# A two-layer block with a dilated attention: the next projection begun inside the feed-forward, groups kept as tops and sums in the order 16, 4, 1, and two token tiles merged inside the last attention

## The chip, the cores and the metric

The kernel runs on one core of one Trainium2 chip. The metric is the device time of one execution in microseconds. The kernel before took 2705.37 us, the median of 3 runs (2704.56 to 2706.03).

## The reference

The input x has 1024 tokens of 1024 float32 values. Two layers follow each other. Layer 0 mixes tokens with a gated linear attention, layer 1 with a dilated window attention; each layer then has a cross attention over 256 memory rows, an output projection, and a feed-forward with a depthwise convolution. What matters here:

```python
def reference(x, mem, positions, ...):
    mem_n = rms_norm(mem, mem_norm)
    for i in range(2):
        h = rms_norm(x, mix_norm[i])
        tok, xq = gla_mixer(h, ...) if i == 0 else dilated_mixer(h, b_w_in, b_q_norm, b_k_norm, positions)
        xa = memory_cross_attention(xq, mem_n, xa_w_kv[i], xa_q_norm[i], xa_k_norm[i])
        x = x + jnp.concatenate([tok, xa], axis=-1) @ w_out          # 512 + 256 columns in layer 1
        x = x + conv_ffn(rms_norm(x, ffn_norm[i]), ffn_w_up[i], ffn_conv_w[i], ffn_conv_b[i], ffn_w_down[i])
    return x

def dilated_mixer(h, w_in, q_norm, k_norm, positions):
    q, k, v, xq = split_cols(h @ w_in, [1536, 1536, 1536, 256])
    q, k = normed and rotated, 12 heads of 128
    for g, (window, dilation) in enumerate(((128, 1), (512, 4), (2048, 16))):     # 4 heads each
        o, lse = dilated_window_attention(q[g], k[g], v[g], window, dilation)     # lse = m + log(l)
    wts = jax.nn.softmax(jnp.stack(lses), axis=0)
    return jnp.sum(wts[..., None] * jnp.stack(outs), axis=0), xq
```

m is the largest score of a row, l the sum of exp(score - m), and o is normalised by l.

## The kernel before

Tokens lie in 8 tiles of 128. Every float32 matrix product is made of three products of rounded parts, high x high, high x low and low x high (`split_matmul`, L50 to L52), so each weight is loaded raw, its high part is copied by the scalar engine (ACT) and its low part subtracted by the vector engine (DVE), or both are made by GpSimd (POOL). The program is a row of phases (`p0`, `gla`, `o0`, `f0`, `p1_0`, `da0`, `p1_1`, `da1`, `p1_2`, `da2`, `o1`, `f1`); each is one block with an instruction stream per engine, written out by hand with semaphores, and ends in a barrier of all engines. So in each phase every engine works in its program's order, and nothing of a phase starts before the one ahead has ended.

`ffn_phase` runs 11 groups. The last one (`down_group`, 16 psum banks of 512 columns, banks 4 to 7 in turn) multiplies the down weights; DVE adds each bank to x (L256), and a bank is used again when it was added four banks later. In `f0` the norm for layer 1 is made beside it: ACT squares and scales a tile (L421, L426), POOL makes the root (L431, L433), PE turns it (L453), DVE applies the gain (L463), ACT makes the high and DVE the low part (L469, L475). The down weights' last parts (L195, L249) come ahead of it.

`project_phase` multiplies the normed rows with blocks of weights, in groups of three token tiles, each block in two halves of rows (`kh`). In a "heads" block ACT squares each head (L982), POOL makes the root (L1015, L1017), DVE scales (L1046) and rotates (L1062 to L1068), PE turns the heads one group later (L1088) and ACT copies them out (L994). A block's weights are split by ACT (L803) and DVE (L808) ahead of the tiles of the last group of the block before; the high part of the first half waits until the last group has read the old ones. The first block of `p1_0` is the memory query of layer 1, 256 columns (its raw weights are loaded during `f0`, and split at the phase's start); then come q, k and v, 512 columns each.

`attention_phase` runs one unit for each token tile and head (32 for a dilated group; `da0` has 32 more for the memory attention): PE makes the scores (L1179), DVE masks them and finds the top (L1208), ACT takes the exponential and its sum (L1230), PE turns the probabilities (L1187), DVE copies them (L1216) and inverts the sum (L1217), PE multiplies with the values (L1196), ACT scales the result with the inverse (L1239). PE turns unit i - 2 and multiplies unit i - 3 while it scores unit i. A group ends with Ln of the sums on ACT (L1242) and a subtraction on DVE (L1220). SP stores the outputs of four units at a time to DRAM, in the order of tokens, and the logarithms (L2278). POOL splits weights for what comes next: two chunks of the next q block, or three of the six chunks of the output projection (L545, L547). The groups run with dilation 1, 4, 16.

`out_phase` of layer 1 (`o1`) splits the other weight chunks, loads the logarithms and, tile by tile, the three groups' outputs, forms the weights (`Merge.dve_weights`, L1965 to L1975) and the weighted sum (`Merge.dve_add`: 4 operations at L1986, 8 at L1988), turns the merged tile (L719), splits it (ACT L625, DVE L665), and multiplies it with the output weights: 36 matmuls of 512 columns a tile. Then it adds x and makes the norm of the feed-forward.

Of the kernel before, what the change touches and what calls it, by code (L numbers as in the profile page):

```python
# [27 lines left out]
P = 128  # L28
# [49 lines left out]
def ffn_phase(nc, ph, psum, ident, neg_half, X, hT_hi, hT_lo, w_up, conv_w, conv_b, w_down, x_out, raws, up, next_gain=None, next_w=None):  # L78
# [3 lines left out]
    with ExitStack() as ctx:  # L82
# [15 lines left out]
        taps_rows = sb("taps_rows", [2 * FC, 4, P])  # L98
        taps = sb("taps", [P, 4, 2 * FC])

# [48 lines left out]
        def _(sp):  # L149
# [19 lines left out]
            for j in range(2 if next_w else 0):  # L169
                sp.wait_ge(up_split, 2 * FC - 2)  # L170
                raws.load(sp, j, next_w[j])
# [6 lines left out]
        def _(act):  # L178
# [44 lines left out]
            high_last_down()  # L223
            if norm:
# [10 lines left out]
        def _(dve):  # L235
# [26 lines left out]
            def group(g, par, last=False):  # L262
# [29 lines left out]
                if not is_first(g):  # L292
                    add_group(g - 1, range(8, 12))
                    if last:
                        low_last_down()
                    add_group(g - 1, range(12, 2 * TT))
# [19 lines left out]
        def _(pe):  # L316
# [52 lines left out]
            if norm:  # L369
                for t in range(TT - LAG, TT):  # L370
                    norm.pe(pe, t)

        for j in range(2):
            raws.count[j] += 16 * (FC - 1 + (next_w is not None))
# [107 lines left out]
class OutWeights:  # L482
# [3 lines left out]
    def __init__(self, nc, ctx, ph, chunks, w_out, raws, ahead):  # L486
# [6 lines left out]
        self.before = list(raws.count)  # L493
        for k in range(chunks):
# [22 lines left out]
    def load_ahead(self, sp, k):  # L517

        if k < min(self.ahead + 2, self.chunks):
            self.load(sp, k)  # L520
# [40 lines left out]
def out_phase(nc, ph, psum, ident, neg_half, XY, weights, x_dram, gain, out_hi, out_lo, w_up, up, raws, stage=None):  # L561
# [3 lines left out]
    with ExitStack() as ctx:  # L565
# [8 lines left out]
        y_hi = [x[:, 0:chunks, :] for x in up.hi]  # L574
        y_lo = [x[:, 0:chunks, :] for x in up.lo]
# [12 lines left out]
        merge = Merge(nc, ctx, ph, stage, XY) if stage is not None else None  # L588
# [3 lines left out]
        def _(sp):  # L592
            for k in range(weights.ahead + 2, (chunks - 1 if merge else chunks) if weights.stage is None else 0):
                weights.load(sp, k)
            if merge:
                stage.wait_logs(sp)
                merge.load_logs(sp)
                stage.wait_outputs(sp)
                merge.load(sp, 0)
                for k in range(max(weights.ahead + 2, chunks - 1), chunks):  # L600
                    weights.load(sp, k)
                merge.load(sp, 1)
            for j in range(2):
# [1920 lines left out]
```

## Time and profile before

| | |
|---|---|
| runs | 2705.37 us median (2704.56 to 2706.03) |
| profiled execution | 2706.76 us, its span 2704.9 us |
| PE matmul busy | 2596.7 us |
| DVE busy | 1317.2 us |
| ACT busy | 845.6 us |
| POOL busy | 185.9 us |

Busy is the time in which the engine has an instruction in work. Matmuls overlap each other, so the distance between the starts of two, and not their duration, is what one costs. A wait row names the instruction that waited, then what ended the wait, and the sum, number and longest of the waits. PEq is PE's own sequencer: a wait put down to it here is the start of a phase.

### The profile page before, as it was taken

Reading aid. Unit: us, or ns where it says so; the run is one execution under the profiler, and the core shown is the slowest. Engines: PE = TensorE matmul, PEld = TensorE weight load, DVE = VectorE, ACT = ScalarE, POOL = GpSimd, SP = SyncE. Lnnn points to the kernel's source line nnn. Section 1 sums busy time; section 2 is a strip of 40 time slices with the busy share of each in tenths; the row PEclk is TensorE's granted clock in tenths of the full one; section 3 lists DMA queues with packets and bytes.
Section 4 is the critical chain, followed back from the end, with each engine's and each line's share of the span. In section 5 each row is a group of like instructions: output and inputs, shape, how many; then the busy total and the mean of one; then the engine's idle time right before and its main releaser. Section 6 shows DMA issues by size and latency. Waiting matters only on the chain. (4 is left out here: it accounts for less than half of the span.)

```text
span 2704.9 us, 33076 instructions
## 1 busy us (share of the span) xinstructions
PE 2596.7 (96%) x12444; PEld 2201.6 (81%) x12444; DVE 1317.2 (49%) x2306; ACT 845.6 (31%) x1782; POOL 185.9 (7%) x263
## 2 busy tenths in 40 slices
PE   7998888999999999998999999997999999999999
PEld 7997767888888888887888888796778888888887
DVE  4423463354445555545545553443645444544455
ACT  6434342332222222224326433324332222222221
POOL 1100120000000000002211111111000000000000
PEclk9999898999999999998999999998999999999999
DMA  4221301131111111102102001103421111111111
GB/s 145 89 71 26 99 6 50 36 96 47 47 47 51 50 47 47 47 32 101 58 6 75 32 32 55 55 16 103 140 65 55 60 49 47 49 52 47 47 39 63
DMA packets 165245, 153.88 MB, mean 57 GB/s; under 512 B 32856, under 2 KB 135496, under 8 KB 165128
## 3 DMA queue, kind: packets, MB, share of 16 engines
q1 hardware_dynamic: 160968, 152.31, 17.7%
q8 instruction: 72, 1.18, 0.2%
q10 hardware_dynamic: 4160, 0.02, 0.1%
q14 instruction: 45, 0.37, 0.1%
HBM read 134.69 MB, written 17.61 MB: 56 GB/s over the span
## 5 line engine op out<-in xcount | busy, mean ns | idle before, releaser
L356 PE MATMUL psum<-hT_hi,f_up_hi 128*128 128x512 f32 x1376 | 426.7, 389 | 4.6 <-PEq L565 3.9
L356 PE MATMUL psum<-hT_hi,f_up_lo 128*128 128x512 f32 x1376 | 426.3, 389 | 0.0
L356 PE MATMUL psum<-hT_lo,f_up_hi 128*128 128x512 f32 x1376 | 426.2, 389 | 0.0
L238 DVE TENSOR_TENSOR f_up_lo<-raw,f_up_hi 128x1024 fp32r<-128x1024 f32 x84 | 102.9, 1225 | 490.6 <-ACT f_up_hi L182 490.6
L356 PEld LDWEIGHTS psum<-hT_hi,f_up_hi 128*128 128x128 f32 x1376 | 258.1, 188 | 59.4 <-issue 5.9
L356 PEld LDWEIGHTS psum<-hT_hi,f_up_lo 128*128 128x128 f32 x1376 | 258.3, 188 | 53.8
L356 PEld LDWEIGHTS psum<-hT_lo,f_up_hi 128*128 128x128 f32 x1376 | 258.3, 188 | 53.6
L256 DVE TENSOR_TENSOR XY<-XY,psum 128x512 f32<-128x512 f32 x352 | 234.4, 684 | 113.9 <-PE psum L52 113.7
L182 ACT ACTIVATE f_up_hi<-raw 128x1024 fp32r<-128x1024 f32 x84 | 89.1, 1061 | 614.6 <-PE psum L356 589.0
L50 PE MATMUL psum<-w_hi,hT_hi 128*128 128x512 f32 (+1 forms) x640 | 250.0, 391 | 17.0 <-DVE w_lo L808 10.5
L50 PE MATMUL psum<-f_down_hi,f_act_hi 128*128 128x512 f32 x640 | 249.0, 389 | 0.0
L51 PE MATMUL psum<-f_down_lo,f_act_hi 128*128 128x512 f32 x640 | 249.0, 389 | 0.0
L52 PE MATMUL psum<-f_down_hi,f_act_lo 128*128 128x512 f32 x640 | 249.0, 389 | 0.0
L52 PE MATMUL psum<-w_hi,hT_lo 128*128 128x512 f32 (+1 forms) x640 | 246.1, 385 | 0.0
L51 PE MATMUL psum<-w_lo,hT_hi 128*128 128x512 f32 (+1 forms) x640 | 246.0, 384 | 0.0
L50 PEld LDWEIGHTS psum<-w_hi,hT_hi 128*128 128x128 f32 x640 | 138.8, 217 | 35.7 <-DVE w_lo L808 10.1
L52 PEld LDWEIGHTS psum<-w_hi,hT_lo 128*128 128x128 f32 x640 | 138.8, 217 | 18.1
L51 PEld LDWEIGHTS psum<-w_lo,hT_hi 128*128 128x128 f32 x640 | 139.1, 217 | 16.7
L52 PEld LDWEIGHTS psum<-f_down_hi,f_act_lo 128*128 128x128 f32 x640 | 120.1, 188 | 25.0
L51 PEld LDWEIGHTS psum<-f_down_lo,f_act_hi 128*128 128x128 f32 x640 | 120.1, 188 | 24.9
L50 PEld LDWEIGHTS psum<-f_down_hi,f_act_hi 128*128 128x128 f32 x640 | 120.1, 188 | 24.9
L50 PE MATMUL psum<-w_hi,h_hi 128*128 128x384 f32 (+1 forms) x320 | 106.1, 332 | 2.3 <-DVE h_lo L475 1.7
(296 smaller groups left out, 4019.5 us busy)
## 6 DMA issues: line engine op xcount, KB each, us to landing
raw<-in_ffn_w_up_dram SPq DMA_DIRECT2D x88, 512.0 KB, 3.7
f_down_raw<-in_ffn_w_down_dram SPq DMA_DIRECT2D x22, 1024.0 KB, 4.9
w_raw<-in_b_w_in_dram SPq DMA_DIRECT2D x18, 1024.0 KB, 5.0
w_raw<-in_a_w_in_dram SPq DMA_DIRECT2D x8, 768.0 KB, 5.8
group_out<-stage SPq DMA_DIRECT2D x24, 256.0 KB, 2.3
o_outs<-group_out SPq DMA_DIRECT2D x24, 256.0 KB, 3.5
XY<-in_x_dram SPq DMA_DIRECT2D x8, 512.0 KB, 10.2
w_raw<-in_xa_w_kv_dram SPq DMA_DIRECT2D x8, 512.0 KB, 3.6
```

Of the source, the lines that this page charges most:

```text
L50: nc.tensor.matmul(out, lhs_hi, rhs_hi, start=start, stop=False)
L51: nc.tensor.matmul(out, lhs_hi, rhs_lo, start=False, stop=False)
L52: return nc.tensor.matmul(out, lhs_lo, rhs_hi, start=False, stop=stop)
L182: nc.scalar.activation(up_hi[n_slot][:, :, :], up_raw[n_slot], ACT.Copy).then_inc(up_high, 1)
L238: nc.vector.tensor_tensor(up_lo[n_slot][:, :, :], up_raw[n_slot], up_hi[n_slot][:, :, :].bitcast(F32), ALU.subtract).then_inc(up_split, 1)
L256: nc.vector.tensor_tensor(xs, xs, psum[:, 4 + i % 4, :], ALU.add).then_inc(x_added, 1)
L356: mm = nc.tensor.matmul(psum[:, 2 * j + half, :], w[j][:, d, :], h[:, d, half * HALF:(half + 1) * HALF], start=first, stop=final)
```

## The change

Three parts.

In `f0` a new helper, `Begun`, loads, splits and holds the memory query's weights, and PE multiplies token tiles 0 to 3 with them in banks 4 to 7 between the last transposes of the norm. `p1_0` finds these four tiles done and computes tiles 4 to 7 with the same weights; its slots for weights now load without waiting for earlier ones.

The dilated groups run in the order 16, 4, 1. Outputs are stored unnormalised, with the tops and the sums in place of the logarithm. Ln, its subtraction and the reciprocals of these units are gone. The weights become exp(-(top - smallest negated top)), divided by the sum over the groups of weight x sum. The last group's tops and sums stay in SBUF.

In the last attention (dilation 1) POOL splits all six chunks of the output weights, the last three after the first tiles' weights are formed. At fixed units DVE forms the weights of token tiles 0 and 1 (units 14 and 16) and merges tile 0 (units 18, 20, 22), PE turns tile 0 into bank 7 (units 10 and 28), and ACT and DVE split it. SP loads the groups' parts of tiles 0 and 1. `out_phase` starts with the matmuls of tile 0 and with the merge of tile 1; SP loads x and the other tiles in a new order.

```diff
@@ ffn_phase
             if norm:
                 for t in range(TT - LAG, TT):
+                    if begin:
+                        if t == TT - LAG:
+                            pe.wait_ge(norm.low, begin.TILES)
+                        for i in begin.between[t - TT + LAG]:
+                            pe.wait_ge(x_added, 2 * TT * GROUPS - begin.TILES + i + 1)
+                            begin.pe(pe, i, psum[:, 4 + i, :], hT_hi, hT_lo)
                     norm.pe(pe, t)
+                for i in begin.between[LAG] if begin else ():
+                    pe.wait_ge(x_added, 2 * TT * GROUPS - begin.TILES + i + 1)
+                    begin.pe(pe, i, psum[:, 4 + i, :], hT_hi, hT_lo)
...
@@ ffn_phase, vector engine
                     if last:
                         low_last_down()
+                        if begin:
+                            begin.low_parts(dve)
                     add_group(g - 1, range(12, 2 * TT))
...
+class Begun:
+    TILES = 4
+    between = ((0,), (1, 2), (3,))
...
+    def pe(self, pe, t, bank, stat_hi, stat_lo):
+        if t == 0:
+            pe.wait_ge(self.split, 2)
+        for d in range(DC):
+            tok = slice(t * P, (t + 1) * P)
+            split_matmul(self.nc, bank[:, 0:self.w.shape[1]], stat_hi[:, d, tok], stat_lo[:, d, tok],
+                         self.hi[d // 4][:, d % 4, :], self.lo[d // 4][:, d % 4, :], d == 0, d == DC - 1)
...
@@ OutWeights
-    def split_ahead(self, pool):
+    def split_ahead(self, pool, merge):
         for k in range(self.ahead):
+            if k == self.ahead // 2:
+                pool.wait_ge(merge.weighed, 1)
...
@@ attention_phase, scalar engine
-                    nc.scalar.activation(out, psum[:, S + T + u % O, 0:w], ACT.Copy, scale=inv[:, u:u + 1]).then_inc(out_done, 1)
-                if i == staged + T_LAG - 1 and staged:
-                    act.wait_ge(inverted, staged)
-                    nc.scalar.activation(total[:, 0:staged], total[:, 0:staged], ACT.Ln).then_inc(logged, 1)
+                    src = psum[:, S + T + u % O, 0:w]
+                    if u < staged:
+                        if u % 4 == 0 and stage.before(u // 4):
+                            act.wait_ge(stage.stored[u // 4 % 2], stage.before(u // 4))
+                        nc.scalar.activation(out, src, ACT.Copy).then_inc(out_done, 1)
...
@@ Merge
+    EARLY = 2
+    TURN_XA, EXP, ADD, TURN = 10, 15, 18, 28
...
+    def dve_ahead(self, dve, i, topped, expd, mixed):
+        if i == self.EXP - 1:
+            dve.wait_ge(topped, self.EARLY * DIL_HEADS)
+            dve.wait_ge(self.logs_loaded, 16 * 2 * (self.G - 1))
+            self.shift(dve, 0, self.EARLY)
+        if i == self.EXP + 1:
+            dve.wait_ge(expd, self.EARLY * DIL_HEADS)
+            self.weigh(dve, 0, self.EARLY)
+        if i == self.ADD:
+            dve.wait_ge(mixed, 2 * DIL_HEADS)
+            dve.wait_ge(self.first_loaded, 16 * 2 * self.G)
+        if self.ADD <= i < self.ADD + 2 * self.G and (i - self.ADD) % 2 == 0:
+            self.add_group(dve, 0, (i - self.ADD) // 2)
+        if i in (self.TURN_XA + 1, self.TURN + 1):
+            part = i == self.TURN + 1
+            dve.wait_ge(self.high, part + 1)
+            self.nc.vector.tensor_tensor(self.turn_rows(self.turn_lo, part), self.turn_cols(part),
+                                         self.turn_rows(self.turn_hi, part).bitcast(F32), ALU.subtract).then_inc(self.low, 1)
...
@@ out_phase, vector engine
             if merge:
-                for k in range(weights.ahead, chunks - 1):
-                    weights.low_part(dve, k)
-                merge.dve_weights(dve)
-                merge.dve_add(dve, 0)
-            y_part(0)
...
+                merge.dve_add(dve, 1)
+                merge.shift(dve, merge.EARLY, TT)
+                merge.weigh(dve, merge.EARLY, TT)
...
@@ build
+        order = [2, 1, 0]
...
-            slots = WeightSlots(nc, slots_ctx, "w", HALF, raws)
+            slots = WeightSlots(nc, slots_ctx, "w", HALF, -2)
```

## Rows read from the trace of the kernel before

**Rows 1.** The page's busy time, share of the span and instructions by engine.
```profile
PE 2596.7 (96%) x12444; PEld 2201.6 (81%) x12444; DVE 1317.2 (49%) x2306; ACT 845.6 (31%) x1782; POOL 185.9 (7%) x263
```

**Rows 2.** Waits of PE, 1190 to 2000 us: total, times, longest.
```profile
PE psum L719 <- DVE XY L1988: 15.6, 1, 15.6
PE psum L50 <- DVE w_lo L808: 10.5, 6, 8.0
PE psum L50 <- PEq L1141: 6.5, 2, 4.8
...
PE psum L1187 <- ACT raw L1230: 2.5, 2, 1.6
PE psum L356 <- PEq L565: 2.2, 1, 2.2
```

**Rows 3.** Windows: busy by engine, PE's granted clock, DMA share, GB/s.
```profile
1248.00:1293.00 45.00, 32.06 (x233) 30.84 (x232) 19.71 (x39) 20.81 (x83) 10.86 (x18) 0.81 0.20 71
1700.00:1705.00 5.00, 4.96 (x15) 4.02 (x16) 0.00 (x0) 0.00 (x0) 0.00 (x0) 0.67 0.44 109
1878.00:1909.00 31.00, 12.71 (x49) 9.87 (x48) 14.23 (x43) 7.99 (x11) 0.00 (x0) 0.67 0.60 180
```

**Rows 4.** Timeline of PE, end of f0 to q block: start, us, instruction.
```profile
1248.39 1.03 PE L453 MATMUL psum<-ident,f_conv_value 128*128 128x128 f32 x8
...
1278.39 0.28 PE L50 MATMUL psum<-w_hi,hT_hi 128*128 128x256 f32 x1
...
1278.75 0.28 PE L50 MATMUL psum<-w_hi,hT_hi 128*128 128x256 f32 x1
...
1292.66 0.47 PE L50 MATMUL psum<-w_hi,hT_hi 128*128 128x512 f32 x1 [1.68 <-DVE w_lo L808]
```

**Rows 5.** Timeline of ACT and DVE, first query tile's head rows.
```profile
1272.47 0.22 ACT L982 ACTIVATE raw<-psum 128x64 f32<-128x64 f32 x1 [9.09 <-PE psum L52]
...
1274.81 0.86 DVE L1046 SCALAR_TENSOR_TENSOR p_head_roped<-psum,p_head_rstd,xa_q_gain 128x64 f32<-128x64 f32 x4 [9.98 <-POOL p_head_rstd L1017]
```

**Rows 6.** Timeline of DVE and PE before f0's last group.
```profile
1217.51 2.35 DVE L249 TENSOR_TENSOR f_up_lo<-f_down_raw,f_up_hi 128x1024 fp32r<-128x1024 f32 x2
...
1222.14 0.39 PE L50 MATMUL psum<-f_up_hi,f_act_hi 128*128 128x512 f32 x1
```

**Rows 7.** Timeline of ACT and SP at the end of da1.
```profile
1696.29 0.35 ACT L1239 ACTIVATE stage<-psum,da_inv 128x128 f32<-128x128 f32 x1
...
1697.03 1.30 SPq L2278 DMA_DIRECT2D group_lse<-stage_lse  x2
```

**Rows 8.** A window of the dilation-1 group, columns as in rows 3.
```profile
1450.00:1461.00 11.00, 11.00 (x83) 9.99 (x82) 8.39 (x41) 8.55 (x30) 4.77 (x2) 1.00 0.16 60
```

**Rows 9.** Timeline of DVE, weights and first merged tile in o1.
```profile
1887.87 0.18 DVE L1965 TENSOR_TENSOR o_top<-o_logs 128x32 f32<-128x32 f32 x1
...
1890.40 0.87 DVE L1986 TENSOR_SCALAR XY<-o_outs,o_logs 128x128 f32<-128x128 f32 x4
1891.31 2.31 DVE L1988 SCALAR_TENSOR_TENSOR XY<-o_outs,o_logs,XY 128x128 f32<-128x128 f32 x8
```

**Rows 10.** Timeline of POOL in da2 and f0, and DVE beside it.
```profile
1850.53 1.04 POOL L545 CAST o_w_hi<-raw 128x1024 fp32r<-128x1024 f32 x1 [51.89 <-DMA raw<-in_b_w_out_dram]
1851.65 2.37 POOL L547 TENSOR_TENSOR o_w_lo<-raw,o_w_hi 128x1024 fp32r<-128x1024 f32 x1
...
1236.43 0.99 POOL L431 TENSOR_SCALAR f_norm_sums<-f_norm_sums 128x1 f32<-128x1 f32 x1 [2.31 <-ACT f_conv_value L421]
...
1236.15 1.22 DVE L475 TENSOR_TENSOR hT_lo<-f_down_raw,hT_hi 128x1024 fp32r<-128x1024 f32 x1
```

**Rows 11.** Timeline of PE, end of da2 and second tile of o1.
```profile
1877.22 0.85 PE L1196 MATMUL psum<-XY,da_buffer 128*128 128x128 f32 x4
...
1909.12 0.50 PE L50 MATMUL psum<-o_w_hi,f_up_hi 128*128 128x512 f32 x1 [0.93 <-DVE f_up_lo L665]
```

**Rows 12.** Chain of waits, 512-column matmuls: start, us, what.
```profile
1997.43 71.03 PE psum L356 x312
```

More of the change, by code:

```diff
@@ L517, in load_ahead @@
     def load_ahead(self, sp, k):
-        if k < min(self.ahead + 2, self.chunks):
-            self.load(sp, k)
+        self.load(sp, k)
     @classmethod
@@ L611, in _ @@
                 sp.dma_start(x_old[:, :], x_dram[t * P:(t + 1) * P, :]).then_inc(x_loaded, 16)
+                if merge and t == 0:
+                    merge.load(sp, 2)
+                    merge.load(sp, 3)
+                if merge and 4 <= t + 3 < TT:
+                    merge.load(sp, t + 3)
+                if t == 2:
+                    for j in range(2):
+                        sp.wait_ge(w_split, chunks)
+                        raws.load(sp, j, up_unit(w_up, j, 0))
         def y_cols(t):
@@ L632, in _ @@
             if merge:
-                for k in range(weights.ahead, chunks - 1):
-                    weights.high_part(act, k)
-                merge.act_exp(act)
-            y_part(0)
-            for k in range(chunks - 1 if merge else weights.ahead, chunks):
+                merge.act_exp(act, merge.EARLY, TT)
+            else:
+                y_part(0)
+            for k in range(weights.ahead, chunks):
                 weights.high_part(act, k)
@@ L811 @@
 class SlotsAhead:
+    ahead_loads = 2
     def __init__(self, slots, w):
@@ L1128, in project_phase, with attention_phase @@
         slots.ahead = 0
-def attention_phase(nc, ph, psum, ident, units, stage=None, loads=(), load_unit=0, ahead=None, room=()):
+def attention_phase(nc, ph, psum, ident, units, stage, loads=(), ahead=None, room=(), merge=None):
     U = len(units)
-    staged = TT * DIL_HEADS if stage is not None else 0
+    staged = TT * DIL_HEADS
     with ExitStack() as ctx:
@@ L1262, in _ @@
             def _(pool):
-                ahead.split_ahead(pool)
-        if staged:
-            stage.groups += 1
+                ahead.split_ahead(pool, merge)
+        stage.groups += 1
+        stage.sums_due = U == staged and not merge
 def head_part(w, h, part):
@@ new lines, in act_exp, with weigh @@
+    def act_exp(self, act, t0, t1):
+        act.wait_ge(self.shifted, 1 if t0 == 0 else 2)
+        self.nc.scalar.activation(self.tops[:, :, t0:t1, :], self.tops[:, :, t0:t1, :], ACT.Exp, scale=-1.0).then_inc(self.expd, 1)
+    def weigh(self, dve, t0, t1):
+        nc, tops, inv = self.nc, self.tops[:, :, t0:t1, :], self.inv[:, t0:t1, :]
+        scaled = self.scaled[:, :, t0:t1, :]
+        dve.wait_ge(self.expd, 1 if t0 == 0 else 2)
+        for g in range(self.G):
+            ins = nc.vector.tensor_tensor(scaled[:, g, :, :], tops[:, g, :, :], self.sums[:, g, t0:t1, :], ALU.mult)
```

426 lines of the change are left out of this document (265 added, 161 removed).

## The prediction

> **What bounds the kernel now.** I read the page's busy line first: TensorE works for 2596.7 of 2704.9 us, the vector engine for half, the scalar engine for a third [rows 1]. So the time can fall only where PE stands idle, runs at its lower clock, or does less. The change removes no matmul (the four query tiles and the transposes that it moves are all still done), so the second view is PE's own waits in the stretch that the change touches, from the end of the first feed-forward to the second one [rows 2]. Of its waiting there, 15.6 us is one wait for the first merged token tile, 10.5 us is for split weights (8.0 of it in one place, right after the feed-forward), 6.5 us is two phase starts of which one is 4.8 us and the other therefore 1.7 us, and 2.5 us is for the scalar engine inside attention. The third view is the windows: in the 45 us after the feed-forward PE is busy for 32.1 us at a mean granted clock of 0.81, and in the 31 us after the last attention for 12.7 us at 0.67 [rows 3]. These two places hold nearly all that can be won.
>
> **Part A, the first feed-forward begins the query projection.** Before: the last down-projection matmul makes room at 1248.39 for the transposes of the norm, and the second block of the projection phase starts at 1292.66, which is 44.3 us later [rows 4]. In it lie three tiles of transposes, the whole 256-column query block (8 tiles), and the waits. After: three times about 1.0 us of transposes (the x8 row), and four query tiles set between them. A tile is 8 row blocks x 3 = 24 matmuls; three of them take 1278.75 - 1278.39 = 0.36 us at full clock, so 2.9 us a tile and 11.5 us for four. They fill PE while norm tiles 6 and 7 are scaled, so those waits go. That is 14.5 us to the end of the feed-forward. Then the phase change, 2.2 us as at the start of the second feed-forward, where PE is also the last to finish [rows 2]. Then the other four tiles: 11.5 us of matmuls, 8 tiles of head transposes of about 0.28 us (2.2 us), and two kinds of wait. The first head rows are now wanted early: from the first square to the end of the scaling is 1272.47 to 1274.81 + 0.86 = 1275.67, so 3.2 us [rows 5], with PE there after 2.9 us, and the second tile 1.3 us behind the first, so 1.3 us of waiting in all. And the block after it still waits for its weights: the scalar engine may begin their high parts only after the last group's first half is read, the same order as now, and now PE waits 1.68 us for it [rows 4]; I take 1.8. Sum 14.5 + 2.2 + 11.5 + 2.2 + 1.3 + 1.8 = 33.5 us, so 10.8 us won.
> Two things go against it. The low parts of the new weights are queued on the vector engine directly behind the two low parts of the last down weights, which take 2.35 us [rows 6]; another 2.35 us moves the adds that free the four down banks from 1219.8 to 1222.1. PE starts the last group at 1222.14 and needs the first of those adds (0.7 us) by then: +0.7. And after the gap the work is less dense than a full block, so the clock may fall for some microseconds: 0 to 1.5, I take 0.7. The high parts cost nothing: the scalar engine made the down weights' ones before 1217.5, and its next work is the square of the first finished tile. The weights' loads stand where they stood. Part A: -9.4, bounds -5 and -12. The weight loads of the next block are now queued without waiting for the query weights' split; they landed before they were needed already, so nothing.
>
> **Part B, tops and sums instead of logarithms.** Each dilated group now ends without the table load, Ln and subtraction. In the group that is followed by the memory attention, PE waited 1.6 us for it [rows 2]: -1.6. In the middle group the last output was scaled behind the Ln, at 1696.29 + 0.35, and then two log stores held SP until 1698.33 [rows 7], and PE started 4.8 us after its last matmul. Without both, the output is ready some 1.0 us earlier and SP is free 1.3 us after that: the gap becomes 2.5, -2.3. After the 4.8 us gap the clock ran at 0.67 of full for 5 us [rows 3], which costs 1.65 us of work; a 1.7 us gap in [rows 2] did without. At 2.5 us I take half: -0.8. The four small stores now go out at the head of SP's queue in the next phase, ahead of weights that are needed 45 us later: nothing. The reciprocals that fall away are on an engine with time to spare in every unit [rows 8]. Part B: -4.7, bounds -3 and -6. The order 16, 4, 1 changes the places and not the number of strided reads: nothing, bounds -1 and +1.
>
> **Part C, the last attention carries two merged tiles.** PE gets 6 transposes there, 0.8 us. The vector engine decides the rest. In 11 us of the dilation-1 group it runs about 40 instructions, four a unit, and is busy for 8.4 us [rows 8]: a unit takes 1.10 us and leaves it 0.26; with the reciprocal gone it is about 0.37. In units 14 to 23 it now gets: shift and weights (about 14 small operations; the same chain for all tiles at once ran from 1887.87 to 1890.40 with three operations fewer and a short wait; at a quarter of the size I take 2.1 us), then 0.87 us and twice 1.15 us of the weighted sum (the rows of four and of eight operations, [rows 9]), so 5.3 us against 10 x 0.37 = 3.7. They come in lumps: the backlog peaks at about 2.8 us behind unit 22, and a unit's scores may be about 0.8 us late before PE sees it. That is 2.0 us of PE waiting. Behind each lump stand the mask of the next unit and the copy of the turned probabilities, and PE waits for both.
> On top of it, GpSimd now splits all six weight chunks in this phase, the last three released by the weights, so they run for 3 x (1.04 + 2.37) = 10.2 us, exactly beside the eight sums that read two SBUF operands. The trace shows the two engines block each other once: a GpSimd operation on one element a partition took 0.99 us from 1236.43, and ended when the vector engine's subtraction from 1236.15 (1.22 us) did [rows 10]. The other direction is not in the trace, since no long GpSimd operation meets such a vector operation. Bounds: 0 if vector operations never wait, 10.2 us if all of it is waited out. I take one and a half waits of 2.37 us, 3.5 us: the row in hand shows one wait per meeting, not one per operation.
> The Trainium skill (SBUF — State Buffer, "SBUF: two separate sides") says that this is an exclusive lock for the whole instruction, taken by whichever starts first, and that a vector operation with two SBUF inputs counts; the row agrees with it. By that rule every one of the eight sums could find a GpSimd operation in front of it, and the sum would go to the upper bound.
> Part C costs 0.8 + 2.0 + 3.5 = +6.3, bounds +1 and +13.
>
> **Part D, the output projection starts at once.** Before: last attention matmul ends at 1877.22 + 0.85 = 1878.07, the second token tile starts at 1909.12, 31.0 us [rows 11]. After: the weights are all split (the weights come at unit 16, some 20 us into a phase of 32 units of 1.10 us and its start, and GpSimd needs 10.2 us from there), tile 0 is turned and split. A gap of 2.6 us (0.4 last output, 0.4 SP's store, 1.7 phase change), then 36 matmuls of 71.03/312 = 0.228 us, 8.2 us [rows 12], and 0.8 us of transposes of tile 1: 11.6 us. The transposes need the merge of tile 1, which is the vector engine's first work, 0.87 + 2.31 = 3.2 us [rows 9], against 4.1 us of matmuls. Behind it stand the other six tiles' weights (about 3 us) and then tile 1's low part, which ends some 9.0 us after the start, as PE gets there: 0.2 us. The later loads are one tile further ahead than now. -19.4 + 0.2 = -19.2, bounds -15 (clock low for the first tile) and -20.
>
> **Sum.** -9.4 - 4.7 + 6.3 - 19.2 = -27.0 us. The profiled execution took 2706.76 us (span 2704.9 and 1.9 around it), so 2679.8; the median of the runs is 1.4 below the profiled one, so 2678.4.
>
> **Rivals.**
> - *The vector engine absorbs the merge* (part C at 1 to 3 us: no lock waits, backlog hidden). For it: 0.37 us to spare in every unit and a wait of PE that no row shows there. Against: 5.3 us of work in ten units. 2678.4 - 4.3 = 2674.
> - *The lock is paid in full* and PE, waiting, drops its clock. 10.2 in place of 3.5, and 1.65 us once or twice: 2678.4 + 6.7 + 2.5 = 2688. For it: GpSimd has no pause between its operations. By the Trainium skill's rule (same page and section) this is the case to expect if each sum waits.
> - *The early query tiles buy little*: the four remaining tiles run at the pace of their head rows, and the clock falls. The block then takes 5 us more: 2683. Against: rows every 1.4 us, matmuls 2.9 us a tile.
> - *Slower than before*: one mechanism in the last attention. All six chunks (6 x 3.41 = 20.5 us) are waited out by a vector engine that is behind, PE idles in every unit, its clock stays at the lower of its two levels (1.2 GHz), and the 18 units from 14 on take 18 x 1.10 = 19.8 us more. 40.3 us are paid and 33.3 won (the sum without part C), so 2712. It decides from 33 us paid. For it: PE waits on the same two vector operations in each unit. Against: the first three chunks are done before the sums begin, and the gap of 4.8 us cost no more than 1.65 us of work [rows 3].
>
> **Chances and range.** Forecast 0.50, absorbed 0.24, lock in full 0.15, little from the early tiles 0.08, slower 0.02, and 0.01 near no change. The first four give 2666 to 2694 with their own spreads; leaving out 2 in 10 gives 2669 to 2689. A change of under 0.2% (5.4 us) can't be told from none here. Faster 0.97, same 0.01, slower 0.02.
>
> **What would show it.** A: in the feed-forward's tail, matmuls of 256 columns between the norm's transposes, no wait over 1 us, and about 33 us instead of 44.3 from the last down matmul to the first matmul of the 512-column block. B: no Ln; PE's gap before the last projection near 2.5 us. C: in the last attention ten units from 14 on take 15 to 19 us in place of 11, with PE's waits in units 16 to 24 on vector-engine rows, and single sums that last over 1 us beside GpSimd rows. D: no wait of over 3 us between the last attention and the second token tile, and 11 to 13 us between them. I am wrong if the last attention's PE waits pass 12 us, if PE still waits for a merged tile in the output phase, or if the clock is low for the whole first token tile.

## The result, and the profile after

The kernel after took 2680.74 us, the median of 4 runs (2676.32 to 2681.2); the kernel before took 2705.7 beside it. The ratio is 0.9901 (95% interval 0.9884 to 0.9919), so 25 us or 1.0% are gone. The forecast was 2678.4 in 2669 to 2689. The profiled execution took 2681.2 us, its span 2679.4.

The page's busy line of the kernel after, against [rows 1]:

```profile
PE 2594.6 (97%) x12444; PEld 2198.9 (82%) x12444; DVE 1313.4 (49%) x2222; ACT 825.4 (31%) x1772; POOL 196.4 (7%) x269
```

PE has the same 12444 matmuls and is busy 2.1 us less than before, so all but 2.1 of the span's 25.5 us were saved in PE's idle time. PE's waits from 1190 to 2000 us, kernel after, against [rows 2]:

```profile
PE psum L1277 <- DVE da_buffer L1299: 6.8, 5, 4.7
PE psum L50 <- PEq L1216: 5.5, 3, 2.0
...
PE psum L50 <- PEq L82: 3.1, 1, 3.1
PE psum L1260 <- PEq L2668: 3.1, 1, 3.1
```

The waits of 15.6 us for the merged tile and of 8.0 us for the split weights are gone, and so is the 4.8 us phase start (the longest is now 3.1). New is the first row: 6.8 us for the copy of the turned probabilities, 6.3 of it in the last attention.

The starts of the stretches, from PE's timeline, kernel after. In order: the last group of `f0`; the projection of tiles 4 to 7; the 512-column block; the first attention; `p1_1`; the middle attention; `p1_2`; the last attention; `o1`; its second tile; `f1`:

```profile
1221.44 0.47 PE L50 MATMUL psum<-f_up_hi,f_act_hi 128*128 128x512 f32 x1 [0.57 <-DVE XY L262]
...
1265.21 0.36 PE L50 MATMUL psum<-f_next_w,hT_hi 128*128 128x256 f32 x1 [3.13 <-PEq L82]
...
1282.14 0.47 PE L50 MATMUL psum<-w_hi,hT_hi 128*128 128x512 f32 x1 [1.34 <-DVE w_lo L867]
...
1426.93 0.58 PE L1260 MATMUL psum<-dil_kT,dil_qT 128*128 128x128 f32 x1 [2.11 <-PEq L929]
...
1494.99 0.77 PE L50 MATMUL psum<-w_hi,hT_hi 128*128 128x512 f32 x1 [1.55 <-PEq L1216]
...
1639.06 0.57 PE L1260 MATMUL psum<-dil_kT,dil_qT 128*128 128x128 f32 x1 [2.11 <-PEq L929]
...
1683.45 0.47 PE L50 MATMUL psum<-w_hi,hT_hi 128*128 128x512 f32 x1 [1.99 <-PEq L1216]
...
1825.75 0.55 PE L1260 MATMUL psum<-dil_kT,dil_qT 128*128 128x128 f32 x1 [3.08 <-PEq L2668]
...
1873.54 0.76 PE L50 MATMUL psum<-o_w_hi,hT_hi 128*128 128x512 f32 x1 [1.99 <-PEq L1216]
...
1884.04 0.39 PE L50 MATMUL psum<-o_w_hi,f_up_hi 128*128 128x512 f32 x1
...
1965.72 0.47 PE L364 MATMUL psum<-hT_hi,f_up_hi 128*128 128x512 f32 x1 [1.75 <-PEq L584]
```

The kernel before, the starts of the first attention, of `p1_1`, and of the last attention:

```profile
1434.49 0.35 PE L1179 MATMUL psum<-dil_kT,dil_qT 128*128 128x128 f32 x1 [2.12 <-PEq L869]
...
1510.12 0.47 PE L50 MATMUL psum<-w_hi,hT_hi 128*128 128x512 f32 x1 [1.69 <-PEq L1141]
...
1846.94 0.58 PE L1179 MATMUL psum<-dil_kT,dil_qT 128*128 128x128 f32 x1 [3.14 <-PEq L2474]
```

The other starts of before are 1292.66, 1909.12 [rows 4, 11], 1652.87 and 1700.05 (middle attention and `p1_2`) and 1991.34 (`f1`). The last group of `f0` began at 1222.14 before and at 1221.44 - 0.57 = 1220.87 after. Then the account is, with each stretch's before and after:

| stretch | before | after | difference |
|---|---|---|---|
| up to the last group of `f0` | 1222.14 | 1220.87 | -1.3 |
| to the 512-column block (part A) | 70.52 | 61.27 | -9.25 |
| the three projections after it | 431.5 | 431.2 | -0.3 |
| first and middle attention | 122.81 | 112.45 | -10.4 |
| last attention, to its last matmul | 31.13 | 45.80 | +14.7 |
| from there to the second token tile (part D) | 31.05 | 12.49 | -18.56 |
| the rest | | | -0.4 |

The groups changed places, so the three attentions are read together: -10.4 + 14.7 = +4.3, which is part B (less) and part C (more).

DVE in the last attention of the kernel after, the first merged tile (rows of x1 and x2 are parts of the four):

```profile
1846.24 5.67 DVE L2118 TENSOR_SCALAR XY<-XY,merge_tops 128x128 f32<-128x128 f32 x4
1846.24 2.22 DVE L2118 TENSOR_SCALAR XY<-XY,merge_tops 128x128 f32<-128x128 f32 x1
1846.24 3.20 DVE L2118 TENSOR_SCALAR XY<-XY,merge_tops 128x128 f32<-128x128 f32 x2
1849.55 2.36 DVE L2118 TENSOR_SCALAR XY<-XY,merge_tops 128x128 f32<-128x128 f32 x1
1853.39 2.87 DVE L2120 SCALAR_TENSOR_TENSOR XY<-XY,merge_tops 128x128 f32<-128x128 f32 x4
1857.66 1.13 DVE L2120 SCALAR_TENSOR_TENSOR XY<-XY,merge_tops 128x128 f32<-128x128 f32 x4
```

GpSimd beside it, kernel after:

```profile
1846.02 2.35 POOL L566 TENSOR_TENSOR o_w_lo<-raw,o_w_hi 128x1024 fp32r<-128x1024 f32 x1
1848.32 1.04 POOL L564 CAST o_w_hi<-raw 128x1024 fp32r<-128x1024 f32 x1
1849.44 2.39 POOL L566 TENSOR_TENSOR o_w_lo<-raw,o_w_hi 128x1024 fp32r<-128x1024 f32 x1
...
1852.97 2.35 POOL L566 TENSOR_TENSOR o_w_lo<-raw,o_w_hi 128x1024 fp32r<-128x1024 f32 x1
```

Four multiplications took 0.87 us before [rows 9] and take 5.67 here. The fourth starts at 1849.55, just behind GpSimd's subtraction of 1849.44, and lasts 2.36; the two end within 0.1 us of each other. The multiply-adds of 1853.39 start inside the next subtraction and take 2.87 in place of the 1.13 of the group behind it, where GpSimd is done. That is 4.8 + 1.7 = 6.5 us of DVE's time.

PE waits 4.69 us for the copy that stands behind the four multiplications. Behind that wait its granted clock was 0.66 for 5 us, which is another 0.34 x 5 = 1.7 us. Window of the kernel after, columns as in [rows 3]:

```profile
1852.86:1857.86 5.00, 4.85 (x21) 4.17 (x22) 4.97 (x14) 2.29 (x11) 2.39 (x2) 0.66 0.01 2
```

### The profile page after: what moved, and what is told of

Same layout as the page of the kernel before. It is cut to its first block and busy times, and to the rows that moved or that the text cites. A ratio compares the mean times of both kernels' runs of the same rounds, so it can differ in the third digit from the quotient of the medians.

```text
span 2679.4 us, 32916 instructions
## 1 busy us (share of the span) xinstructions
PE 2594.6 (97%) x12444; PEld 2198.9 (82%) x12444; DVE 1313.4 (49%) x2222; ACT 825.4 (31%) x1772; POOL 196.4 (7%) x269
## 5 line engine op out<-in xcount | busy, mean ns | idle before, releaser
L50 PE MATMUL psum<-w_hi,hT_hi 128*128 128x512 f32 x576 | 230.0, 399 | 5.7 <-PEq L1216 3.5
L52 PE MATMUL psum<-w_hi,hT_lo 128*128 128x512 f32 x576 | 226.8, 394 | 0.0
L51 PE MATMUL psum<-w_lo,hT_hi 128*128 128x512 f32 x576 | 226.6, 393 | 0.0
L50 PEld LDWEIGHTS psum<-w_hi,hT_hi 128*128 128x128 f32 x576 | 125.2, 217 | 23.9 <-issue 5.3
L52 PEld LDWEIGHTS psum<-w_hi,hT_lo 128*128 128x128 f32 x576 | 125.3, 218 | 18.0
L51 PEld LDWEIGHTS psum<-w_lo,hT_hi 128*128 128x128 f32 x576 | 125.5, 218 | 16.8
```

Of the source, the lines that this page charges most:

```text
L50: nc.tensor.matmul(out, lhs_hi, rhs_hi, start=start, stop=False)
L51: nc.tensor.matmul(out, lhs_hi, rhs_lo, start=False, stop=False)
L52: return nc.tensor.matmul(out, lhs_lo, rhs_hi, start=False, stop=stop)
```

## The experiments

Time before the last group of `f0` differs between profiled runs by up to 6.0 us (last section), so each kernel is also read over the stretch that the change touches, from the last group of `f0` to the first matmul of `f1`: 769.2 us before, 744.9 after. "Last attention" is from its first score to the first output matmul.

| kernel | median us | ratio (95%) | that stretch | part A | last attention |
|---|---|---|---|---|---|
| after | 2680.74 | 0.9901 (0.9884 to 0.9919) | 744.9 | 61.27 | 47.79 |
| after, again | 2679.92 | 0.9905 (0.9888 to 0.9921) | 744.5 | 61.31 | 47.88 |
| sums later | 2678.44 | 0.9890 (0.9873 to 0.9906) | 740.6 | 61.31 | 42.67 |
| GpSimd behind the sums | 2676.20 | 0.9879 (0.9863 to 0.9896) | 740.4 | 61.30 | 42.67 |
| multiply-adds first | 2683.25 | 0.9900 (0.9884 to 0.9917) | 747.4 | 61.26 | 49.57 |
| one sum of twelve | 2674.12 | 0.9880 (0.9863 to 0.9896) | 737.6 | 61.29 | 41.03 |
| tiles later | 2687.08 | 0.9929 (0.9912 to 0.9946) | 751.7 | 68.57 | 47.80 |
| Ln back | 2692.95 | 0.9948 (0.9932 to 0.9965) | 757.4 | 61.28 | 50.23 |
| stores only | 2686.50 | 0.9925 (0.9908 to 0.9941) | 750.5 | 61.28 | 48.13 |
| order 4, 16, 1 | 2684.08 | 0.9918 (0.9901 to 0.9934) | 747.6 | 61.30 | 48.08 |
| spread, on ACT | 2673.74 | 0.9871 (0.9854 to 0.9887) | 740.1 | 61.30 | 41.79 |
| all, and tile order | 2676.45 | 0.9890 (0.9874 to 0.9907) | 736.7 | 60.82 | 41.80 |

### What the last attention pays for: four kernels

The question was whether its extra time is DVE waiting for GpSimd ("the port" in the expectations), or plain load on DVE.

**Sums later.** Units 25, 27, 29 in place of 18, 20, 22, when GpSimd is nearly done.

```diff
-    TURN_XA, EXP, ADD, TURN = 10, 15, 18, 28
+    TURN_XA, EXP, ADD, TURN = 10, 15, 25, 31
```

> The changed kernel with the twelve weighted sums of token tile 0 moved from units 18, 20, 22 to units 25, 27, 29 of the last attention, and its turn from unit 28 to 31. By then GpSimd has finished its last three weight chunks. The work and the amount left to each engine are the same. Theory P (the shared port: each sum waits for a whole GpSimd operation): the four multiplications take about 0.9 us instead of 5.7 and the eight sums 2.3 instead of 4.0, PE's one wait of 4.7 us in the last attention goes, and the kernel takes 5 to 7 us less than the changed one: about 2674. Theory V (the vector engine simply has more work than it has time for beside the units): the same wait comes at the later units, 0 to 1 us won: about 2680.

**GpSimd behind the sums.** Its last three chunks wait for the sums; SP loads the last of them after tile 5's store.

```diff
@@ split_ahead
-                pool.wait_ge(merge.weighed, 1)
+                pool.wait_ge(merge.added, 1)
@@ attention_phase, SP
-                if ahead is not None and 2 + t < ahead.ahead_loads:
-                    ahead.load_ahead(sp, 2 + t)
+                k = 2 + t if t < 3 else (5 if t == 5 else DC)
+                if ahead is not None and k < ahead.ahead_loads:
+                    ahead.load_ahead(sp, k)
```

> The changed kernel with the sums where they are (units 18, 20, 22) and GpSimd's last three weight chunks held back until tile 0 is merged instead of until its weights are formed; the load of the last chunk goes behind the store of tile 5. Theory P: the multiplications take 0.9 us, PE's wait of 4.7 us goes; but GpSimd's 10.2 us then end at about the end of the phase and can hold the phase change by 0 to 3 us: 2 to 6 us won, 2675 to 2679. Theory V: PE's waits stay near 6 us in the attention, and the late end of GpSimd comes on top: 2681 to 2684.

**Multiply-adds first.** The four multiplications in the form of the multiply-adds, with a tile of zeros.

```diff
-            if g == 0:
+            if g == 0 and t == 0:
+                ins = nc.vector.scalar_tensor_tensor(Y[:, t, cols], o, w, self.zeros[:, 0:DIL_DIM], ALU.mult, ALU.add)
+            elif g == 0:
...
```

> The changed kernel with the four multiplications of tile 0 (one SBUF tensor and a scalar a partition) written as the form that multiplies and adds a second tensor, here of zeros, so that they read two SBUF tensors. GpSimd works beside them as before. It asks whether the long operations (5.7 us for four) come with the form with one tensor. If the form is what waits each time: four take 2 to 3 us, as the next four did (2.9 us), and 2 to 4 us are won. If it is only that GpSimd was busy when they came, as theory P has it for any operation on the shared port: about 5.7 us again and no difference within 1 us. Theory V: 0.3 us slower, as this form takes 0.28 us instead of 0.20 each.

**One sum of twelve.** The kernel leaves out eleven of the twelve operations that merge tile 0, so its output is wrong; it only gives their price.

```diff
+            if t == 0 and (g < 2 or h < 3):
+                continue
...
```

> The changed kernel without eleven of the twelve weighted sums of token tile 0 in the last attention (they are left out; one stays, as it carries the signal). The weights are formed, everything else stays. This prices the sums, the lock included. Theory P: the vector engine loses 9.7 us of busy time there, PE waits under 1 us after unit 17 and keeps its clock: 7 to 8 us less than the changed kernel, about 2673. Theory V: the part that PE sees is the excess over its slack, 2 us: about 2679.

DVE with GpSimd's chunks behind the sums:

```profile
1847.64 0.86 DVE L2119 TENSOR_SCALAR XY<-XY,merge_tops 128x128 f32<-128x128 f32 x4
...
1850.07 1.13 DVE L2121 SCALAR_TENSOR_TENSOR XY<-XY,merge_tops 128x128 f32<-128x128 f32 x4
1852.60 1.13 DVE L2121 SCALAR_TENSOR_TENSOR XY<-XY,merge_tops 128x128 f32<-128x128 f32 x4
```

PE's waits for DVE in that kernel, 1824 to 1880 us:

```profile
PE psum L1277 <- DVE da_buffer L1299: 1.6, 3, 0.8
```

The same twelve operations at the same units take their bare time once GpSimd is elsewhere, and PE's waits on DVE fall from 6.3 us (four, the longest 4.69) to 1.6. Mere load would have shown no gain in either of the first two kernels.

The column "last attention" falls by 5.12 us in both. That they are equal is chance: the first microseconds of the phase ran at different clocks, before anything that the edits touch. Windows of 7.5 us from the first score, the kernel after and then GpSimd behind the sums:

```profile
1825.75:1833.25 7.50, 7.43 (x40) 6.37 (x41) 4.50 (x22) 4.98 (x21) 3.88 (x3) 0.78 0.66 148
```

```profile
1825.80:1833.30 7.50, 7.43 (x30) 6.25 (x31) 3.61 (x19) 3.75 (x16) 3.83 (x3) 0.58 0.73 150
```

The 0.20 between them is 1.5 us. So the column is split at the first score of unit 18, in front of the first sum:

| kernel | first score to unit 18 | unit 18 to the first output matmul |
|---|---|---|
| after | 18.67 | 29.12 |
| sums later | 18.74 | 23.93 |
| GpSimd behind the sums | 20.04 | 22.63 |
| multiply-adds first | 18.74 | 30.83 |
| one sum of twelve | 18.76 | 22.27 |
| spread, on ACT (below) | 18.73 | 23.06 |

With GpSimd out of the way and the sums in their place, 29.12 - 22.63 = 6.5 us go: about 4.7 of PE's waits and the 1.7 of low clock behind the longest. The sums that then meet nobody cost 22.63 - 22.27 = 0.4 us there; seven units later they cost 1.7, and PE's waits on DVE are 3.0 us instead of 1.6.

With the multiplications as multiply-adds they still wait, all four of them; the row of that kernel:

```profile
1848.97 6.79 DVE L2118 SCALAR_TENSOR_TENSOR XY<-XY,merge_tops,zeros 128x128 f32<-128x128 f32 x4
```

So it is not the form of the instruction that makes them wait. The lone sum left in the kernel with one of twelve, beside a GpSimd subtraction that began at 1848.26, took 1.06 us in place of 0.28:

```profile
1849.71 1.06 DVE L2122 SCALAR_TENSOR_TENSOR XY<-XY,merge_tops 128x128 f32<-128x128 f32 x1
```

The medians follow less closely than the traces. Against the kernel after they are 2.3 us lower for the sums later (5 to 7 expected), 4.5 for GpSimd behind the sums (2 to 6), 6.6 for one sum of twelve (7 to 8), and 2.5 higher for the multiply-adds first (within 1 expected). In the first, second and last of these the three projections took 434.3, 433.0 and 434.3 us against 431.2, at a lower clock behind their gaps (last section).

### Part A in two halves

**Tiles later.** The split stays in `f0`, the four query tiles go back behind the phase change.

```diff
 class Begun:
-    TILES = 4
-    between = ((0,), (1, 2), (3,))
+    TILES = 0
+    between = ((), (), ())
...
```

> The kernel after the change, with part A cut in half: the query weights are still loaded, split and kept in the first feed-forward, but no query tile is multiplied there; the next phase multiplies all eight tiles. Kernel after: 61.27 us from the last group's first matmul to the 512-column block; before: 70.52. Theory of the prediction (the gain comes from matmuls that stand where PE waited for norm tiles and for the phase change, the split weights alone save only what DVE's low part cost at the phase's start): PE waits again for tiles 6 and 7 (0.8 and 2.5 us), the phase starts some 3 us earlier than before, so the stretch is 67 to 68.5 us and the time 2687 (2685 to 2689). Rival 1 (the 8.0 us wait for the split weights was the whole loss, the early tiles only move work): stretch 61 to 63, time 2681. Rival 2 (the early split is worth nothing, the wait was the end of the norm): stretch 70 to 71, time 2690.

Waits of PE in this kernel, 1180 to 1300 us:

```profile
PE psum L50 <- PEq L82: 5.8, 1, 5.8
PE psum L470 <- ACT f_conv_value L443: 2.5, 1, 2.5
PE psum L50 <- DVE w_lo L867: 1.7, 1, 1.7
PE psum L470 <- ACT f_conv_gate L443: 0.8, 1, 0.8
```

68.57 us, against 70.52 and 61.27: the early split alone brings 1.95, the early tiles 7.3. The 8.0 us wait "for the weights" in [rows 2] was mostly the end of the norm and the phase change; with the weights ready, 5.8 us of it stands there under another name, the phase's start. The median is 6.3 above the kernel after. Both rivals are out.

### Part B: Ln, stores, order

**Ln back.** Ln and subtraction in the first two groups, stores behind them.

```diff
+                if i == staged + T_LAG - 1 and not merge:
+                    act.wait_ge(expd, staged)
+                    nc.scalar.activation(logs[:, :], group_sum, ACT.Ln).then_inc(logged, 1)
...
-            if U > staged:
-                sp.wait_ge(expd, staged)
+            if not merge:
+                sp.wait_ge(lse_done, 1)
                 stage.store_sums(sp)
...
-        stage.sums_due = U == staged and not merge
+        stage.sums_due = False
```

> The kernel after the change, with the logarithm's work put back at the end of the first two groups: ACT's Ln of the sums, DVE's subtraction, and SP stores the two small arrays at the end of the same phase behind the subtraction (the results are not used; the reciprocals and the scaling of outputs stay away). Theory of the prediction (Ln's table loads and the stores were what PE waited for): about +1.6 us at the start of the memory attention's units and +2.8 us in the gap before the last projection (1.99 back to 4.8), with part of the low clock after it, so 2680.7 + 4.4 = 2685 (2684 to 2687). Rival (the gap was the last output's scaling with the inverse and its wait for the reciprocal): at most +1, 2681, with a gap of 2.0 to 2.5 us.

**Stores only.** The same without Ln: SP stores the middle group's tops and sums before the phase ends.

```diff
-            if U > staged:
+            if not merge:
                 sp.wait_ge(expd, staged)
                 stage.store_sums(sp)
...
-        stage.sums_due = U == staged and not merge
+        stage.sums_due = False
```

> The kernel after the change, with only the stores put back: SP stores the tops and the sums of the middle group at the end of its own phase (four small stores) and not at the head of the next; no Ln. It splits the 4.0 us that Ln and stores together added there (gap 1.99 to 6.00). Theory: SP's issue of the four stores, 2.6 us, stands behind the last output's store, so the gap is 4.6, the stretch from the middle attention's start to the projection 47.0 (44.4 after), and the first attention is unchanged at 67 to 68; Ln was the other 1.4 us. The time is 2.6 us plus up to 1.6 us of low clock above the kernel after. Rival (it was Ln's table load alone, the stores run beside the barrier): gap 2 to 2.5.

SP at the end of the middle attention with the stores only, and the matmul that follows:

```profile
1681.35 1.29 SPq L2468 DMA_DIRECT2D group_top<-stage_sums  x2
1682.69 1.32 SPq L2468 DMA_DIRECT2D group_sum<-stage_sums  x2
```

```profile
1685.59 0.76 PE L50 MATMUL psum<-w_hi,hT_hi 128*128 128x512 f32 x1 [4.94 <-PEq L1216]
```

The two store rows last 2.6 us behind the last output's store, and the gap is 4.94 in place of 1.99: the stores alone are +3.0 of the 4.05 that Ln and stores add there; Ln is the other 1.0. In the first attention the stores are harmless (67.3 us) and Ln costs 3.5 us (71.5 against 68.06; 4.1 against the 67.4 of the kernel after run again). The median with the stores only is 5.8 us above the kernel after, where 2.6 to 4.2 was expected: `p1_2` took 145.2 us in place of 142.3, its first 5 us at a granted clock of 0.50. ACT in the first attention, with Ln back:

```profile
1457.99 1.28 ACT L1335 ACT_TABLE_LOAD   x1
1459.28 0.23 ACT L1335 ACTIVATE da_logs<-stage_sums 128x32 f32<-128x32 f32 x1
1459.53 1.28 ACT L1319 ACT_TABLE_LOAD   x1
```

PE waits 1.9 us for what is behind the second load; then its clock is lower, in windows of that kernel:

```profile
1456.20:1461.20 5.00, 3.40 (x22) 2.56 (x20) 3.17 (x17) 4.69 (x10) 0.00 (x0) 1.00 0.13 49
1461.20:1466.20 5.00, 4.72 (x24) 4.16 (x25) 2.25 (x10) 3.49 (x15) 0.00 (x0) 0.71 0.20 64
```

0.29 x 5 = 1.45 us of clock, and the sum is about 3.5. I expected +4.4 in all and the median rose by 12.2: 7.5 in the two attentions, 2.3 in `p1_2` and 2.4 in the last attention. The projection begins at half clock, more than the "part of the low clock" that was expected:

```profile
1690.30:1695.30 5.00, 4.96 (x12) 3.92 (x13) 0.00 (x0) 0.00 (x0) 0.00 (x0) 0.50 0.35 24
```

The 2.4 us in the last attention have a second price of Ln in them that neither the prediction nor the expectation had: behind the middle group's Ln, the next attention starts with a table load of 1.28 us in front of its first exponential. The kernel after has no such load there, the kernel before has one at 1846.9. Of the 2.4 us, 1.85 lie ahead of unit 18, this load and a lower clock together:

```profile
1834.92 1.28 ACT L1319 ACT_TABLE_LOAD   x1 [2.40 <-PEq L2677]
```

**Order 4, 16, 1.**

```diff
-        order = [2, 1, 0]
+        order = [1, 2, 0]
```

> The kernel after the change with the groups in the order 4, 16, 1 in place of 16, 4, 1. Theory of the prediction (the order of the first two groups is neutral): within 1 us of the kernel after, 2680.7 (2679.5 to 2682). Rival (the strided token order of dilation 16 costs something that the place hides, as the loads of the first merged tile or the stores ahead of the memory attention): 2 to 4 us either way, and the phases' lengths change by other than their exchange.

The two attentions together take 111.7 us against 112.5: they exchange their times (79.0 and 32.7 for 68.1 and 44.4). The time is nevertheless some 3 us more, outside what I expected, and it lies in the projections: 434.3 against 431.2, 2.9 of it in `p1_2`, which here began at half clock behind the same 2.0 us gap:

```profile
1681.80:1686.80 5.00, 4.96 (x12) 3.94 (x13) 0.00 (x0) 0.00 (x0) 0.00 (x0) 0.50 0.64 201
```

Neither theory had that. Whether the order brings it about, or chance does, one trace can't tell; the four runs' median stands 3.3 above the kernel after, with intervals that overlap.

### Two versions beyond the change

**Spread, on ACT.** As GpSimd behind the sums; ACT makes the four multiplications at unit 17, DVE two multiply-adds a unit from 18 to 21.

```diff
...
+        if i == self.ADD - 1:
+            act.wait_ge(self.weighed, 1)
+            act.wait_ge(self.first_loaded, 16 * 2 * self.G)
+            for h in range(DIL_HEADS):
+                cols = slice(h * DIL_DIM, (h + 1) * DIL_DIM)
+                ins = self.nc.scalar.activation(self.Y[:, 0, cols], self.room[:, h // 2, h % 2 * DIL_DIM:(h % 2 + 1) * DIL_DIM],
+                                                ACT.Copy, scale=self.tops[:, 0, 0, h:h + 1])
+            ins.then_inc(self.scaled_first, 1)
...
```

> As the kernel with GpSimd's last three chunks behind the sums (2676.2), and the sums made lighter and smoother for DVE: ACT makes the four multiplications of the first group at unit 17, and the eight multiply-adds stand two to a unit in units 18 to 21 in place of four in units 20 and 22. Theory (what is left of the last attention's extra time is DVE's lump: PE waits of 0.5 and 0.8 us): the stretch from the last attention's start to the first output matmul falls from 42.7 to 41.8, time 2675.3. Rival (what is left is the weights' chain, the transposes and the clock, as with nearly no sums it was 41.0): the same 42.5 to 42.7, 2676. Second rival (ACT's four operations delay the exponentials): 43.5, 2677.

41.79 us, as expected to the tenth, but by luck: from unit 18 on this kernel takes 23.06 us and GpSimd behind the sums 22.63, and PE's waits on DVE are 2.0 us and 1.6. The 0.9 us came from the clock at the start of the phase, ahead of the edit; spreading the sums gained nothing that the trace shows. The median 2673.74 has a range of 2668.56 to 2678.08.

**All, and tile order.** The same with the early query tiles in another order.

```diff
...
-    between = ((0,), (1, 2), (3,))
+    between = ((0,), (1,), (2, 3))
```

> The best version so far (GpSimd's last chunks behind the sums, four multiplications on ACT, the sums spread over four units) with one more edit in the first feed-forward: the four early query tiles stand as 0; 1; 2 and 3 between the norm's transposes, in place of 0; 1 and 2; 3. In the kernel after the change the last transposes start at 1258.17, 2.9 us (one tile) later than their rows need, DVE ends the low part of the last tile behind them at 1262.5, and PE's gap before the next phase is 3.13 us. Theory (the gap is the norm's end on DVE): with the transposes one tile earlier PE is the last to finish, the gap falls to 2.1 to 2.3 us, the time to 2673 (0.9 less than the version without). Rival (the gap is what a phase change behind the feed-forward takes whoever ends last, or PE then waits for tile 7's scaled rows): gap or new wait of 3 us in sum, no gain.

```profile
1269.61 0.35 PE L50 MATMUL psum<-f_next_w,hT_hi 128*128 128x256 f32 x1 [2.67 <-PEq L82]
```

The gap fell by 0.46 of the 0.9 expected; no new wait came. Beside it the kernel after ran once more:

> The kernel after the change itself, unchanged, on the same chip as the version with all edits, so that the two can be compared directly. Expected: ratio 0.990 to before again, 2680 to 2682, with the last attention's stretch at 47.8 us, the gap before the query block at 3.1, and the version with all edits 7 us below it.

Over the touched stretch this version is the shortest that computes all: 736.7 against 744.5, 7.9 us less, of which 6.1 lie in the last attention. The medians show 3.5 of it (2676.45 and 2679.92; 2673 and a distance of 7 were expected), and the intervals of the ratios overlap; its profiled run came to the last group of `f0` 5.6 us later. The trace shows the gain, the timing does not yet prove it. That it stands 3.4 us below the version without the tile order is 2.9 us of projections (431.4 and 434.3), which are clock, and 0.5 of the edit.

## Why the prediction was right

- **Part A, -9.4 forecast, -9.25 measured.** The stretch without the early tiles shows the mechanism: they fill the waits for norm tiles 6 and 7 and hide the norm's end. The terms: the add's delay 0.57 (0.7 taken), the wait for the block's weights 1.34 (1.8), head rows 0.39 (1.3), the phase start 3.13 (2.2). The last was under-sized, and so was the low clock, 0.7 taken: it was 0.66 for 5 us from 1265.2, so 1.7. Of the 9.25 us, 7.5 are PE's waits (12.9 us in the stretch before, 5.4 after). The norm's tile 7 is turned at 1258.17, one query tile later than its rows need, so DVE and not PE ends the feed-forward.
- **Part B, -4.7 forecast, about -4.4 and -0.3 in the projections measured.** The first attention's wait of 1.6 is gone, as forecast (with Ln put back it costs 3.5 there, clock included); the gap fell by 2.8 (2.3 forecast), to 1.99. The sum of both is -4.4. The forecast's low clock (0.8 saved) did come off ahead of `p1_2`, but came on ahead of `p1_1`; the three projections together changed by 0.3. The two causes I named for the gap weigh 1.0 (Ln) and 3.0 for four stores, so for the two stores of before about half of that, an estimate. What was left out is the table load that Ln brings to the start of the next attention.
- **Part C, +6.3 forecast, +8.7 measured.** The dilation-1 group alone, as the first attention of before: 75.63 - 1.6 (Ln) - 36.9 (its memory units: 68.06 of the kernel after less the 31.13 of the dilation-16 group) = 37.1 us; it is 45.80 now. The term that was mis-sized is the lock, 3.5 taken: it costs PE 6.5 us, about 4.7 in waits and 1.7 in the low clock behind them, which the sum had left to a rival. I counted one and a half waits for the phase; DVE waited 2.0, 0.8 and 2.1 us in the first, second and fourth multiplication, which I had left out of the operations that can wait, and 1.7 in the first multiply-add. The backlog, 2.0 taken, was over-sized: the sums alone cost 0.4 us at these units, and the weights and transposes together 41.03 - 1.99 - 37.1 = 1.9 (0.8 taken for the transposes). 1.9 + 0.4 + 6.5 = 8.8. The rule of the Trainium skill (SBUF — State Buffer, "SBUF: two separate sides") that the shared pair of ports is held for a whole instruction fits every one of these rows; it also lists vector operations in a two-port mode, which the prediction did not weigh. In which mode the multiplications ran no run shows; as multiply-adds with two SBUF inputs they waited too. The cost did not come to the upper bound, because only operations that fall inside a GpSimd one wait, and behind the last chunk nothing does.
- **Part D, -19.2 forecast, -18.56 measured.** The gap is 1.99 (2.6 taken, though its three terms add up to 2.5), the clock was 0.86 in the mean from 1871.5 to 1884, which is 0.14 x 12.5 = 1.75 us, no wait for a merged tile is left. No experiment tested this part alone.
- The rivals: *absorbed* needed 1 to 3 us in part C and is out; *in full* (10.2 us of lock waited out) is out by half, at 4.7, but its second mechanism, the clock that falls behind PE's wait, did happen once; *early tiles buy little* is out by their 7.3 us; the slower one was far.

The sum: part A came out 0.15 above its term, C 2.4 and D 0.6, and the stretches outside the parts 1.7 below (1.3 ahead of them, 0.4 behind). That leaves 1.4 us between the profiled 2681.2 and the 2679.8 forecast for it. So close a sum is partly luck: part C's miss of 2.4 us was offset by 1.3 us ahead of the last group of `f0`, where profiled runs differ by up to 6.0 us.

## What to carry to other kernels

When work is moved beside another engine, list every pair of instructions that will then overlap on a shared resource, count the meetings one by one, and place the heavy one where the other has nothing: here one wait on another semaphore gave 6.5 us of the last attention, clock included, and seven units' shift 5.2. A wait's name in the profile tells what came last, not what a repair will save: with the split weights ready, 2 of the 8 us went, and only work put into the gap brought it to 3.1. Four small stores at the end of the middle attention, 2.6 us of SP's time, held the phase change by 3.0 us; at the head of the next phase no cost of them was seen.

## What the runs showed of the hardware that was not expected

- GpSimd's cast, with one input, holds DVE up too: the first two multiplications end at 1846.24 + 3.20 = 1849.44, the first alone at 1848.46, so the second took 1 us where one alone takes 0.22, beside the cast of 1848.32 to 1849.36.
- Behind the same gap of 1.99 us the granted clock of the next 5 us was 1.00 in the kernel after, 0.66 with GpSimd behind the sums, and 0.50 (1.2 GHz, the lower of the two levels, throughout) in the order 4, 16, 1. `p1_2` took 142.3, 143.9 and 145.2 us in them, so they cost 0, 1.6 and 2.9 us. The windows of the first two of them:

```profile
1683.50:1688.50 5.00, 5.00 (x22) 4.15 (x23) 0.00 (x0) 0.00 (x0) 0.00 (x0) 1.00 0.23 10
```

```profile
1681.90:1686.90 5.00, 5.00 (x15) 3.96 (x16) 0.00 (x0) 0.00 (x0) 0.00 (x0) 0.66 0.23 10
```

  The code of the window is the same. A term for the clock behind a gap of 2 us is thus a chance and no number, and single differences under 3 us between kernels should be read stretch by stretch.
- The 5.6 us by which profiled runs differ ahead of the change lie in layer 0, where PE waits often: from 220 to 534 us the mean granted clock was 0.93 in the kernel after run again, and 0.91 in the version with all edits; the second came to the end of that stage 5.0 us later. The windows, that kernel after and then the version with all edits:

```profile
220.00:534.00 314.00, 285.04 (x1434) 231.41 (x1435) 145.47 (x224) 125.06 (x256) 35.88 (x46) 0.93 0.15 45
```

```profile
220.00:534.00 314.00, 286.96 (x1420) 233.60 (x1421) 146.65 (x224) 124.73 (x256) 35.47 (x46) 0.91 0.15 45
```
